# A decoder trunk with eight experts: expert stages of 2048 and 1536 features in place of 1024 and 512

## Chip, cores and metric

One core of one Trainium2 chip. The metric is the device time of one execution in microseconds; the figure for a kernel is the median of its timed runs. All arithmetic is float32.

## The reference

Two decoder layers over 256 tokens of width 1024. Each layer has a token mixer (four groups of four heads, one input and one output projection) and a channel mixer; layer 0 has a dense SwiGLU, layer 1 the expert SwiGLU that this case is about. Its part of the reference, cut to what is computed:

```python
logits = xf @ router_w + router_b                 # 256 x 8
top_logit, top_e = top_k(logits, 2); top_w = softmax(top_logit)
for each expert e, for the tokens xb that chose it:
    y = (silu(xb @ wg[e]) * (xb @ wu[e])) @ wd[e]  # wg, wu 1024 x 3584; wd 3584 x 1024
    out[token] += top_w * y
x = x + g2 * out
```

Each expert's three matrices are 14.7 MB each, so the eight experts have 352 MB of weights, and each byte is used once.

## The kernel before

**Teams.** After the router the experts are ordered by how many tokens chose them and put into eight slots of five teams (`TEAMS`, line 304): teams 0, 2 and 4 hold two experts side by side in the 128 rows of the PE array's output, teams 1 and 3 one expert. A matmul of a two-expert team is done in `lanes` of 32 or 64 rows, each lane with its own expert's weights; the lanes of one 128 x 512 product run beside each other. The rows of a team are gathered from the normalised activations by a matmul with a 0/1 matrix (`gather`) into `xT`, one of two buffers, and the results are returned to the tokens by a matmul with the transposed, weighted matrix (`moe_scatter`, line 1604), which DVE adds to the residual (`add_team`).

**Stages.** The 3584 features of a team are cut by `SPANS` into stages of 1024, 1024, 1024 and 512 features, that is 2, 2, 2 and 1 units of 512. `STAGES` is the order of the work: the stages of teams 0 and 1 alternate, then those of 2 and 3, then team 4 by itself, 20 stages. In stage j PE does: the gate sums of stage j (`moe_up(j, 0)`), with the transposes of stage j-1's products (`moe_turn`) and other small jobs (`beside`) between the pieces; the up sums (`moe_up(j, 1)`); then the down product of stage j-1 (`moe_down`), summed in banks 0 and 1 over a team's consecutive stages. Where the other team comes next, DVE takes the sums out (`run_out`) into `ysum`.

**Banks and the chain between engines.** The gate sums of a stage's two units stand in banks 4 and 2, the up sums in banks 5 and 3, transposes in 6, gathers and returns in 7. ACT takes tanh of the gate sum (`sigmoid`, line 1028), DVE multiplies it with the gate sum into `hbuf` (`gated`, 2273), and later with the up sum (`multiplied`, 2282); PE transposes `hbuf` into bank 6, ACT copies it to `hbT` (`turned_in`, 1019) for the down product. Gate and up of stage j both wait until all products of stage j-1 are made (semaphore `h`).

**Weights.** All weights come over one queue, SP's, into a ring of seven slots of 2 MB (16 KB on each of 128 partitions). `MOE_LOADS` lists the 168 expert loads in the order in which PE uses them. A gate or up load of a 2-unit stage is a piece of 512 rows by 1024 features (2 MB, runs of 4 KB); for a 1-unit stage it is all 1024 rows by 512 features (runs of 2 KB); a down load is 512 rows of 4 KB that lie together, so that each partition reads one run of 16 KB. SP waits for `ring_free` of the slot, then issues:

```python
sp.wait_ge(ring_free[slot], FREED[slot] + n // RING)
...
sp.dma_start(wide_at(slot), w[512 * piece:512 * piece + 512, st.f0:st.f0 + 1024]...)   # 2 units
sp.dma_start(view_at(slot, 512), w[:, st.f0:st.f0 + 512]...)                          # 1 unit
```

PE frees the slot of a first piece and of a down load with its last matmul on it; ACT frees gate's last piece when the gate sum is done, DVE up's. The very last down load of each of the two last experts is split into two halves, the second on semaphores of its own. The order of the experts is a result of the router, so no expert load is issued before that (`order_ready`).

**Returns.** `RETURN_IN` puts the four returns of each of teams 0 to 3 beside stages 9, 10, 17 and 18; team 4's come after the last stage, in four banks. Experts with more tokens than their slot has rows would be done in a loop at the end (`n_over`).

Of the kernel before, what the change touches and what calls it, by code (L numbers as in the profile page):

```python
# [15 lines left out]
ALU = mybir.AluOpType  # L16
# [281 lines left out]
def expert_steps(rounds):  # L298

    return [Step(w, 0, 0, [3 * u + p for p in range(3)], rounds, True, True, u == 0, u == 6)  # L300
            for u, (_, w) in enumerate(FE_UNITS)]
# [4 lines left out]
SPANS = ((0, 2), (1024, 2), (2048, 2), (3072, 1))  # L306
# [41 lines left out]
GATHER_A, GATHER_B = {2: (6, 2), 3: (8, 0), 4: (14, 2)}, {2: (7, 1), 3: (8, 2), 4: (15, 1)}  # L348
RETURN_IN = {9: 0, 10: 1, 17: 2, 18: 3}
PICKED_IN, WEIGHED_IN, TURNED_IN = {5: (2, 3), 13: (4,)}, {11: (2, 3), 13: (4,)}, {1: (0, 1), 11: (2, 3), 13: (4,)}  # L350
# [3 lines left out]
def _list_loads():  # L354
# [16 lines left out]
assert len(MOE_LOADS) == LOADS * N_EXP  # L371
# [21 lines left out]
def program(nc, t, out):  # L393
    ctx = ExitStack()
    with ctx:
# [108 lines left out]
        pickT_area = [acc[:, 1, :], bias[:, :, :].rearrange("p h n -> p (h n)")[:, 1024:1536]]  # L504
        pickT = [pickT_area[q // 2][:, 256 * (q % 2):256 * (q % 2) + 256].rearrange("p (t n) -> p t n", t=TT) for q in range(4)]
# [3 lines left out]
        ysum = [ysb, bias_flat[:, 0:1024]]  # L509
# [9 lines left out]
        def prm(l, name, p0=0, p1=128):  # L519
# [91 lines left out]
            "g", "u", "tanh", "h", "T", "T_evac", "d", "y_taken", "onehot", "turned", "turn_evac", "gathered", "in_act", "in_vec",  # L611
            "y_0", "y_1", "scattered", "added", "act_seq", "vec_seq", "act_left",
            "vec_left")} for p in ("moe", "over"))
# [26 lines left out]
        def wide_at(slot):  # L640
            return ring[:, slot, :].rearrange("p (k n) -> p k n", k=KC // 2)
# [36 lines left out]
        def _(sp):  # L678
# [82 lines left out]
            for n, (st, part, piece, m) in enumerate(MOE_LOADS):  # L761
# [4 lines left out]
                if part == 2:  # L766
                    src, c = down_rows(e, st, piece, (0,) if st is STAGES[-1] else (0, 1))
                    sp.dma_start(ring[:, slot, c], src).then_inc(ring_full[slot], 16)
                elif st.units == 2:
                    sp.dma_start(wide_at(slot), w[512 * piece:512 * piece + 512, st.f0:st.f0 + 1024].rearrange("(k p) n -> p k n", p=128)).then_inc(ring_full[slot], 16)  # L770
                else:
                    sp.dma_start(view_at(slot, 512), w[:, st.f0:st.f0 + 512].rearrange("(k p) n -> p k n", p=128)).then_inc(ring_full[slot], 16)  # L772

            for m in STAGES[-1].members:
                src, c = down_rows(expert_id(len(TEAMS) - 1, m), STAGES[-1], 0, (1,))
                sp.dma_start(ring[:, moe_slot(STAGES[-1], 2, 0, m), c], src).then_inc(ada_full[m], 16)
# [3 lines left out]
            with sp.If(n_over > 0):  # L780
                with sp.Fori(0, OVER) as i:
                    with sp.If(i < n_over):
                        e = sp.value_load(overi[0:1, bass.ds(i + (OVER + 1), 1)], min_val=0, max_val=N_EXP - 1)
                        for u in range(7):
                            for j in range(3):
                                expert_load(3 * u + j, e, u, j, i * 3 + 3 * N_EXP)
# [18 lines left out]
        def _(act):  # L805
# [213 lines left out]
            def turned_in(j, unit):  # L1019
# [6 lines left out]
                do(act.activation(hbT[:, unit, :], ps[6][:, :], ACT.Copy), moe["T_evac"])  # L1026

            def sigmoid(j, unit):
# [3 lines left out]
                if unit == st.units - 1:  # L1032
                    for m in st.members:
                        act.sem_inc(ring_free[moe_slot(st, 0, st.units - 1, m)], 1)
                if j and unit == 0:
                    act.wait_ge(moe["h"], st.at)
                do(act.activation(hsigs[unit], ps[(4, 2)[unit]][:, :], ACT.Tanh, scale=0.5), moe["tanh"])  # L1037

            for j in range(len(STAGES) + 1):
                if j:  # L1040
                    turned_in(j - 1, 0)
# [3 lines left out]
                if j and STAGES[j - 1].units == 2:  # L1045
                    turned_in(j - 1, 1)
# [18 lines left out]
        def _(pe):  # L1065
# [475 lines left out]
            def moe_up(j, part, between=None):  # L1541
# [5 lines left out]
                if j:  # L1547
                    pe.wait_ge(moe["h"], st.at)
                for piece in range(2):
                    if piece < st.units:  # L1550
                        moe_loaded(pe, st, part, piece)
                    for unit in range(st.units):
                        b = ps[((4, 2), (5, 3))[part][unit]]
                        for k in range(4 * piece, 4 * piece + 4):
                            for n, (m, c0, c1) in enumerate(st.lanes):
                                if st.units == 2:
                                    w = wide_at(moe_slot(st, part, piece, m))[:, k % 4, 512 * unit:512 * unit + 512]
                                else:
                                    w = view_at(moe_slot(st, part, 0, m), 512)[:, k, :]
                                last = mm(b[c0:c1, :], xT[st.team % 2][:, k, c0:c1], w, start=k == 0, stop=k == KC - 1)  # L1560
                                if st.units == 2 and piece == 0 and unit == 1 and k == 3 and n == st.last_lane[m]:
                                    last.then_inc(ring_free[moe_slot(st, part, 0, m)], 1)
                        if piece:
# [4 lines left out]
            def moe_turn(j, unit):  # L1568
# [5 lines left out]
                for q in range(4):  # L1574
                    c = slice(q, 512, 4)
                    last = nc.tensor.transpose(ps[6][:, 128 * q:128 * q + 128], hbuf[:, unit, c], ident)  # L1576
                last.then_inc(moe["T"], 1)

            def moe_down(j):
# [4 lines left out]
                for unit in range(st.units):  # L1584
# [3 lines left out]
                    for qs in ((0, 1), (2, 3)) if st is STAGES[-1] else ((0, 1, 2, 3),):  # L1588
# [3 lines left out]
                        for half in range(2):  # L1592
                            for q in qs:
                                for n, (m, c0, c1) in enumerate(st.lanes):
                                    slot = moe_slot(st, 2, unit, m)
                                    last = mm(ps[half][c0:c1, :], hbT[:, unit, 128 * q + c0:128 * q + c1],  # L1596
# [846 lines left out]
```

## Time and profile before

| | us |
|---|---|
| median of 3 runs | 1579.42 |
| lowest, highest | 1575.38, 1581.16 |
| the profiled execution | 1575.83 |
| its span, first to last instruction | 1574.0 |
| mean granted TensorE clock | 0.975 of full speed |
| PE busy | 1466.0 (93%) |
| DVE busy | 471.2 (30%) |
| ACT busy | 197.6 (13%) |
| HBM read | 479.41 MB, 305 GB/s over the span |

Busy shares are means over stages with different limits. The expert part runs from about 695 us, where the order of the experts is known, to about 1563 us; the rest of the time is the first layer and the second mixer, in which the change touches nothing. Times in the rows count from the first instruction.

### The profile page before, as it was taken

The numbers are of one execution on the slowest core, as the hardware profiler recorded it, in microseconds if no ns is written. First come the engines' busy times: TensorE is split into PE (matmuls) and PEld (weight loads), VectorE is DVE, ScalarE is ACT, GpSimd is POOL, SyncE is SP. The second block draws the span as 40 slices with busy tenths as digits, with TensorE's granted clock in tenths as the row PEclk, the third lists the DMA queues.
The fourth block names the chain that finished last, engine by engine and source line by source line (L and its number), as shares of the span: only waits on it lengthen the run. The fifth ranks groups of instructions, "written<-read, shape, count | busy, mean of one in ns | idle before, by whom it ended". The sixth has DMA issues, their size and how long they took to land.

```text
span 1574.0 us, 16822 instructions
## 1 busy us (share of the span) xinstructions
PE 1466.0 (93%) x6928; PEld 720.5 (46%) x6928; DVE 471.2 (30%) x937; ACT 197.6 (13%) x427; POOL 2.5 (0%) x23
## 2 busy tenths in 40 slices
PE   6899999999999999988989999999999999987886
PEld 2576755555544756662424333434343344332322
DVE  4478725344334555352100111112110110110001
ACT  1123223000003132330000000100000001000000
POOL 0000000000000000000000000000000000000000
PEclk9999989999999999989999999999999999999999
DMA  9935535887874310039999999999999999999995
GB/s 345 360 136 182 187 112 197 270 299 247 310 280 151 108 55 1 1 115 409 419 414 419 408 417 404 411 411 419 411 418 409 413 409 410 411 409 418 418 401 225
DMA packets 151647, 481.60 MB, mean 306 GB/s; under 512 B 15848, under 2 KB 33640, under 8 KB 144144
## 3 DMA queue, kind: packets, MB, share of 16 engines
q1 hardware_dynamic: 150120, 478.64, 78.4%
q10 hardware_dynamic: 1448, 1.84, 0.4%
q8 instruction: 57, 0.93, 0.2%
q14 instruction: 22, 0.18, 0.0%
HBM read 479.41 MB, written 1.06 MB: 305 GB/s over the span
## 4 chain that ended last, share of the span: by engine, by line
PE 77%; DMA 17%; DVE 2%; SPq 1%; ACT 1%; issue 1%; DVEq 0%; ACTq 0%
PE bank L1560 23%; PE bank L1596 14%; DMA ring<-in_moe_wu 13%; PE bank L1432 9%; PE bank L1190 7%; PE bank L1450 5%; PE bank L1179 4%; PE bank L1397 3%; DMA ring<-in_moe_wg 2%; DMA ring<-in_ada_w 1%; PE bank L1317 1%; PE bank L1169 1%; SPq L772 1%; PE bank L1267 1%; PE bank L1266 1%
## 5 line engine op out<-in xcount | busy, mean ns | idle before, releaser
L1560 PE MATMUL bank<-ring,h_T 128*32 128x512 f32 (+1 forms) x2240 | 310.2, 614 | 47.4 <-DMA ring<-in_moe_wu 35.3
L1596 PE MATMUL bank<-ring,m_qk_T 128*32 128x512 f32 (+2 forms) x1344 | 246.7, 596 | 12.6 <-issue 10.0
L1560 PEld LDWEIGHTS bank<-ring,h_T 128*32 128x32 f32 (+1 forms) x2240 | 99.8, 118 | 244.5 <-issue 243.4
L1560 PE MATMUL bank<-ring,cmp_region 128*128 128x512 f32 x448 | 196.3, 592 | 1.2 <-DVE m_s_region L2289 1.2
L1596 PEld LDWEIGHTS bank<-ring,m_qk_T 128*32 128x32 f32 (+2 forms) x1344 | 88.6, 128 | 166.4 <-issue 166.4
L1432 PE MATMUL bank<-ring,h_T 128*128 128x384 f32 (+1 forms) x448 | 156.8, 503 | 0.7 <-DVE m_s_region L2088 0.7
L1560 PEld LDWEIGHTS bank<-ring,cmp_region 128*128 128x128 f32 x448 | 84.0, 190 | 102.0 <-issue 102.0
L1190 PE MATMUL bank<-ring,h_T 128*128 128x512 f32 (+1 forms) x320 | 119.1, 522 | 0.8 <-ACT wide L879 0.5
L1432 PEld LDWEIGHTS bank<-ring,h_T 128*128 128x128 f32 x448 | 83.3, 190 | 61.3 <-issue 15.5
L1026 ACT ACTIVATE m_qk_T<-bank 128x512 f32<-128x512 f32 x35 | 20.9, 597 | 656.4 <-PE bank L1576 655.9
L2289 DVE SCALAR_TENSOR_TENSOR m_s_region<-m_s_region,bank 128x512 f32<-128x512 f32 x35 | 24.1, 688 | 262.1 <-PE bank L1560 262.1
L1190 PEld LDWEIGHTS bank<-ring,h_T 128*128 128x128 f32 x320 | 60.7, 196 | 43.5 <-issue 38.3
L1450 PE MATMUL bank<-ring,m_qk_T 128*128 128x512 f32 x176 | 77.9, 593 | 0.7 <-ACT m_qk_T L982 0.7
L2179 DVE SCALAR_TENSOR_TENSOR ada_acc<-ring,cond,ada_acc 128x512 f32<-128x512 f32 x98 | 73.7, 752 | 5.0
L2280 DVE SCALAR_TENSOR_TENSOR m_s_region<-s_v,bank 128x512 f32<-128x512 f32 x20 | 13.8, 688 | 155.5 <-ACT s_v L1037 155.5
L1179 PE MATMUL bank<-h_T,ring 128*128 128x256 f32 x256 | 60.3, 390 | 0.0
L1397 PE MATMUL bank<-ring,h_T 128*128 128x512 f32 x128 | 59.7, 615 | 0.0
L1179 PEld LDWEIGHTS bank<-h_T,ring 128*128 128x128 f32 x256 | 48.7, 195 | 7.7 <-ACT m_s_region L881 0.7
L1450 PEld LDWEIGHTS bank<-ring,m_qk_T 128*128 128x128 f32 x176 | 33.4, 190 | 40.2 <-issue 36.4
L2150 DVE TENSOR_TENSOR x_res<-bank,x_res 128x512 f32<-128x512 f32 x20 | 13.8, 692 | 96.0 <-PE bank L1612 95.5
L1397 PEld LDWEIGHTS bank<-ring,h_T 128*128 128x128 f32 x128 | 24.2, 197 | 25.8 <-issue 25.8
L948 ACT ACTIVATE prob<-prob,neg_max 128x128 f32<-128x128 f32 (+1 forms) x48 | 21.8, 455 | 88.5 <-DVE neg_max L1900 87.7
(355 smaller groups left out, 1041.5 us busy)
## 6 DMA issues: line engine op xcount, KB each, us to landing
ring<-in_moe_wg SPq DMA_DIRECT2D x56, 2048.0 KB, 21.2
ring<-in_moe_wu SPq DMA_DIRECT2D x56, 2048.0 KB, 21.2
ring<-in_moe_wd SPq DMA_DIRECT2D x54, 2048.0 KB, 23.1
ring<-in_ada_w SPq DMA_DIRECT2D x28, 1024.0 KB, 8.8
ring<-in_ada_w SPq DMA_DIRECT2D x10, 2048.0 KB, 14.2
ring<-in_w_in SPq DMA_DIRECT2D x10, 2048.0 KB, 10.7
ring<-in_ffn_wg SPq DMA_DIRECT2D x6, 1536.0 KB, 10.2
ring<-in_ffn_wu SPq DMA_DIRECT2D x6, 1536.0 KB, 9.0
```

The source lines that it names most:

```text
L772: sp.dma_start(view_at(slot, 512), w[:, st.f0:st.f0 + 512].rearrange("(k p) n -> p k n", p=128)).then_inc(ring_full[slot], 16)
L948: do(act.activation(e[:, a:b], e[:, a:b], ACT.Exp, bias=nmax[:, i % 4, tt:tt + 1], accum_out=lsum[:, i // H, h, tt:tt + 1]), head_exp if t ...
L1026: do(act.activation(hbT[:, unit, :], ps[6][:, :], ACT.Copy), moe["T_evac"])
L1179: last = mm(b[:, 256 * part:256 * part + 256], w[:, k, 128 * (2 * g + part):128 * (2 * g + part) + 128], hT[:, k, :], start=k == 0, stop=k ...
L1190: last = mm(b[:, 0:cols], hT[:, k, 128 * tt:128 * tt + 128], w[:, k, c0:c0 + cols], start=k == 0, stop=k == KC - 1)
L1397: last = mm(b[:, :], hT[:, k, 128 * tt:128 * tt + 128], slot_view(i, 512)[:, k, :], start=k == PAIRS_OF_K[0][0], stop=k == PAIRS_OF_K[3][1])
L1432: last = mm(ps[5 - part if f is ffn else 4 + part][:, 0:w], hT[:, k, 128 * st.tile:128 * st.tile + 128], view_at(slot, w)[:, k, :], start= ...
L1450: last = mm(ps[st.y + half][:, :], hbT[:, j % 2, 128 * q:128 * q + 128], down_at(st.slots[2], st.w)[:, q, 512 * half:512 * half + 512], st ...
L1560: last = mm(b[c0:c1, :], xT[st.team % 2][:, k, c0:c1], w, start=k == 0, stop=k == KC - 1)
L1596: last = mm(ps[half][c0:c1, :], hbT[:, unit, 128 * q + c0:128 * q + c1], down_at(slot, 512)[:, q, 512 * half:512 * half + 512], start=st.b ...
L2179: ins = STT(a, w, cond[:, 4 * i + k:4 * i + k + 1], a, ALU.mult, ALU.add)
L2289: do(STT(hbuf[:, unit, :], hbuf[:, unit, :], 0.5, ps[(5, 3)[unit]][:, :], ALU.mult, ALU.mult), moe["h"])
```

## The change

- `SPANS` has two stages for a team, of 4 and 3 units. There are 10 stages: 0 to 3 for teams 0 and 1, 4 to 7 for teams 2 and 3, 8 and 9 for team 4.
- Gate and up of every stage come in four pieces (`PIECES`) of 256 rows by all features of the stage: 2 MB in runs of 8 KB, or 1.5 MB in runs of 6 KB. Down loads are as before. There are 184 expert loads, and still seven slots.
- Gate and up sums of a unit use one bank (`GU` = 4, 2, 5, 3). PE starts a unit's up sum only after the semaphore `t`, which DVE raises when `gated` has read the gate sum. Up no longer waits for `h`.
- Four buffers each for the products and their transposes, in tiles that are idle in this part; the tanh of units 2 and 3 reuses the buffers of 0 and 1 after `t`.
- The returns of teams 0 and 1 move beside stage 8, those of teams 2 and 3 beside stage 9; each team has a `ysum` of its own until then. Gathers and the making of 0/1 matrices move with the new stage numbers.
- The loop for overfull experts starts at another ring slot (`SHIFT`).

```diff
-SPANS = ((0, 2), (1024, 2), (2048, 2), (3072, 1))
+SPANS = ((0, 4), (2048, 3))
+PIECES = 4
...
-GATHER_A, GATHER_B = {2: (6, 2), 3: (8, 0), 4: (14, 2)}, {2: (7, 1), 3: (8, 2), 4: (15, 1)}
-RETURN_IN = {9: 0, 10: 1, 17: 2, 18: 3}
+GATHER_A, GATHER_B = {2: (2, 4), 3: (4, 0), 4: (6, 4)}, {2: (3, 1), 3: (4, 4), 4: (7, 1)}
+RETURNS = {(j, hook): [(2 * (j - 8) + n // 4, n % 4) for n in pieces]
+           for j in (8, 9) for hook, pieces in enumerate(((0,), (1,), (2,), (3,), (4, 5), (6, 7)))}
+YSUM_OF = (0, 1, 2, 3, 0)
...
-                for piece in range(STAGES[j].units):
+                for piece in range(PIECES):
                     add(STAGES[j], part, piece)
...
+        hbufs = [hbuf[:, 0, :], hbuf[:, 1, :], gate[:, 0, 0:512], gate[:, 0, 512:1024]]
+        hbTs = [hbT[:, 0, :], hbT[:, 1, :], cmp_region[:, 1024:1536], cmp_region[:, 1536:2048]]
+        GU = (4, 2, 5, 3)
...
+                    sp.dma_start(wide_at(slot, st.units), w[256 * piece:256 * piece + 256, st.f0:st.f0 + 512 * st.units].rearrange("(k p) n -> p k n", p=128)).then_inc(ring_full[slot], 16)
...
-                if j and unit == 0:
+                if unit >= 2:
+                    act.wait_ge(moe["t"], st.at + unit - 1)
+                elif j:
                     act.wait_ge(moe["h"], st.at)
-                do(act.activation(hsigs[unit], ps[(4, 2)[unit]][:, :], ACT.Tanh, scale=0.5), moe["tanh"])
+                do(act.activation(hsigs[unit % 2], ps[GU[unit]][:, :], ACT.Tanh, scale=0.5), moe["tanh"])
...
-                if j:
+                if j and part == 0:
                     pe.wait_ge(moe["h"], st.at)
...
+                for piece in range(PIECES):
+                    moe_loaded(pe, st, part, piece)
                     for unit in range(st.units):
-                        b = ps[((4, 2), (5, 3))[part][unit]]
-                        for k in range(4 * piece, 4 * piece + 4):
+                        if part and piece == 0:
+                            pe.wait_ge(moe["t"], st.at + unit + 1)
+                        b = ps[GU[unit]]
+                        for k in range(2 * piece, 2 * piece + 2):
...
-                do(STT(hbuf[:, unit, :], hsigs[unit], 1.0, ps[(4, 2)[unit]][:, :], ALU.add, ALU.mult))
+                do(STT(hbufs[unit], hsigs[unit % 2], 1.0, ps[GU[unit]][:, :], ALU.add, ALU.mult), moe["t"])
```

## Rows read from the trace of the kernel before

**Rows 1.** The page's slices of 39.4 us (PE's busy tenths, granted clock, DMA, GB/s):

```profile
PE   6899999999999999988989999999999999987886
...
PEclk9999989999999999989999999999999999999999
DMA  9935535887874310039999999999999999999995
GB/s 345 360 136 182 187 112 197 270 299 247 310 280 151 108 55 1 1 115 409 419 414 419 408 417 404 411 411 419 411 418 409 413 409 410 411 409 418 418 401 225
```

**Rows 2.** Who waits for whom (us in total, times, longest), PE's and SP's rows:

```profile
PE bank L1560 <- DMA ring<-in_moe_wu: 35.3, 15, 4.6
...
PE bank L1560 <- DMA ring<-in_moe_wg: 12.1, 8, 2.6
...
PE bank L1596 <- DMA ring<-in_moe_wd: 1.8, 1, 1.8
...
PE bank L1560 <- DVE m_s_region L2289: 1.2, 1, 1.2
...
SPq L770 <- PE bank L1560: 106.1, 19, 10.1
SPq L770 <- PE bank L1596: 88.5, 16, 7.0
SPq L770 <- DVEq L2288: 64.2, 12, 9.3
...
SPq L770 <- ACTq L1034: 47.0, 9, 7.7
```

**Rows 3.** Windows: stretch, length, busy us and counts of each engine, clock, DMA share, GB/s:

```profile
core 0: us, PE busy (x) PEld busy (x) DVE busy (x) ACT busy (x) POOL busy (x), PEclk, DMA share, GB/s
697.00:1556.00 859.00, 796.89 (x4344) 315.46 (x4344) 113.69 (x225) 50.94 (x90) 0.00 (x0) 0.98 1.02 411
705.00:745.00 40.00, 31.79 (x261) 12.37 (x264) 9.64 (x30) 3.02 (x6) 0.00 (x0) 0.91 1.02 409
755.00:775.00 20.00, 20.00 (x57) 9.71 (x56) 2.44 (x4) 2.39 (x4) 0.00 (x0) 1.00 1.02 428
970.00:980.00 10.00, 10.00 (x100) 2.99 (x92) 1.38 (x2) 0.00 (x0) 0.00 (x0) 1.00 1.05 387
1546.00:1549.00 3.00, 1.61 (x8) 0.74 (x10) 0.00 (x0) 0.00 (x0) 0.00 (x0) 1.00 1.02 423
5.00:6.00 1.00, 0.00 (x0) 0.00 (x0) 0.00 (x0) 0.00 (x0) 0.00 (x0) 1.00 0.99 401
```

**Rows 4.** Times from issue to landing, line 770: the first load, then 710 to 1500 us:

```profile
L770 SPq DMA_DIRECT2D ring<-in_moe_wg x1: 397/397/397, 695.6 to 695.6; - x1
...
DMA to landing us min/median/max: 7.6/7.6/7.6
...
L770 SPq DMA_DIRECT2D ring<-in_moe_wu x47: 372/2699/6452, 705.1 to 1461.7; - x47
...
L770 SPq DMA_DIRECT2D ring<-in_moe_wg x44: 372/384/6004, 722.7 to 1441.8; - x44
...
DMA to landing us min/median/max: 11.4/21.8/29.0
```

**Rows 5.** Chain of waits in order: start, us, what (counts include weight loads):

```profile
696.76 13.01 DMA ring<-in_moe_wg
...
764.22 13.74 PE bank L1560 x32
777.96 13.87 PE bank L1596 x128
...
849.40 0.47 PE bank L1576 x4
849.87 6.87 PE bank L1560 x16
...
992.43 1.98 PE bank L1497 x16
...
1015.48 1.78 PE bank L1497 x16
...
1087.95 0.86 PE bank L1612 x2
...
1234.54 8.77 PE bank L1560 x64
...
1424.68 7.10 PE bank L1560 x32
```

**Rows 6.** Groups by line, 697 to 1556 us: names, count, busy us, mean ns, idle:

```profile
L1026 ACT ACTIVATE m_qk_T<-bank 128x512 f32<-128x512 f32 x35 | 20.9, 597 | 656.4 <-PE bank L1576 655.9
...
L2280 DVE SCALAR_TENSOR_TENSOR m_s_region<-s_v,bank 128x512 f32<-128x512 f32 x20 | 13.8, 688 | 155.5 <-ACT s_v L1037 155.5
L1037 ACT ACTIVATE s_v<-bank 128x512 f32<-128x512 f32 x20 | 11.9, 597 | 83.7 <-PE bank L1560 83.7
L2150 DVE TENSOR_TENSOR x_res<-bank,x_res 128x512 f32<-128x512 f32 x16 | 11.1, 692 | 95.1 <-PE bank L1612 94.7
```

**Rows 7.** The same chain at its end:

```profile
1547.39 7.09 PE bank L1596 x32
1554.47 0.69 PE bank L1576 x4
...
1555.25 0.60 ACT m_qk_T L1026
...
1555.99 7.09 PE bank L1596 x32
1563.08 3.65 PE bank L1612 x8
```

More of the change, by code:

```diff
@@ L1044, in _ @@
                         sigmoid(j, unit)
-                if j and STAGES[j - 1].units == 2:
-                    turned_in(j - 1, 1)
+                for unit in units[PIECES - 1:]:
+                    turned_in(j - 1, unit)
                 for team, (at, _) in GATHER_A.items():
@@ L1546, in moe_up @@
                     pe.wait_ge(moe["in_vec"], st.team + 1)
-                if j:
+                if j and part == 0:
                     pe.wait_ge(moe["h"], st.at)
-                for piece in range(2):
-                    if piece < st.units:
-                        moe_loaded(pe, st, part, piece)
+                for piece in range(PIECES):
+                    moe_loaded(pe, st, part, piece)
                     for unit in range(st.units):
-                        b = ps[((4, 2), (5, 3))[part][unit]]
-                        for k in range(4 * piece, 4 * piece + 4):
+                        if part and piece == 0:
+                            pe.wait_ge(moe["t"], st.at + unit + 1)
+                        b = ps[GU[unit]]
+                        for k in range(2 * piece, 2 * piece + 2):
                             for n, (m, c0, c1) in enumerate(st.lanes):
[L1556 to L1563, printed above, removed]
+                                slot = moe_slot(st, part, piece, m)
+                                last = mm(b[c0:c1, :], xT[st.team % 2][:, k, c0:c1], wide_at(slot, st.units)[:, k % 2, 512 * unit:512 * unit + 512],
+                                          start=k == 0, stop=k == KC - 1)
+                                if piece < PIECES - 1 and unit == st.units - 1 and k % 2 and n == st.last_lane[m]:
+                                    last.then_inc(ring_free[slot], 1)
+                        if piece == PIECES - 1:
                             last.then_inc(moe["gu"[part]], 1)
@@ L1574, in moe_turn @@
                 for q in range(4):
-                    c = slice(q, 512, 4)
-                    last = nc.tensor.transpose(ps[6][:, 128 * q:128 * q + 128], hbuf[:, unit, c], ident)
+                    last = nc.tensor.transpose(ps[6][:, 128 * q:128 * q + 128], hbufs[unit][:, q:512:4], ident)
                 last.then_inc(moe["T"], 1)
@@ L1587, in moe_down @@
                     end = st.end and unit == st.units - 1
-                    for qs in ((0, 1), (2, 3)) if st is STAGES[-1] else ((0, 1, 2, 3),):
+                    for qs in ((0, 1), (2, 3)) if st is STAGES[-1] and end else ((0, 1, 2, 3),):
                         if qs[0]:
@@ L1644, in _ @@
                     moe_up(j, 1)
-                    beside(j, 2)
+                    beside(j, 4)
                 else:
-                    moe_turn(j - 1, 0)
+                    for unit in range(STAGES[-1].units):
+                        moe_turn(j - 1, unit)
                 if j:
@@ L1650, in _ @@
                 if j < len(STAGES):
-                    beside(j, 3)
+                    beside(j, 5)
             for n in range(4):
@@ L2130, in run_out @@
                     c = slice(512 * half, 512 * half + 512)
-                    y = ysum[st.team % 2][:, c]
+                    y = ysum[YSUM_OF[st.team]][half]
                     if half:
```

87 lines of the change are left out of this document (44 added, 43 removed).

## The prediction

> **What bounds the kernel now.** I read the page's 40 slices first [rows 1]: from slice 18 on, which is the expert part, the DMA row stands at 9 with some 410 GB/s in every slice but the last, while PE is at 8 or 9 too. Two candidates, so the next view is who waits for whom in this stretch [rows 2]: PE waits for weight loads 35.3 + 12.1 + 1.8 us and for almost nothing else, and SP, which issues the loads, waits far longer for PE, ACT and DVE to free a ring slot. So the loads run ahead until the seven slots are full, and the question is whether the queue ever runs dry. It doesn't: from 697 to 1556 us the rate is 411 GB/s with a DMA share of 1.02 [rows 3], and between 710 and 1500 us a gate or up load takes 11.4 to 29.0 us from issue to landing, where the first one, with nothing ahead of it, took 7.6 [rows 4]; there is always more than one load in the queue. 352.3 MB of expert weights at 411 GB/s are 857 us. PE needs less: one unit of 512 features costs 24 matmuls of 0.86 us and a transpose, 6.87 + 6.87 + 6.93 + 0.47 = 21.1 us [rows 5], whether the team has one expert or two, since the strips of two experts run side by side; 35 units are 739 us. The expert part is bound by its loads, from first to last, and PE has 100 us to spare in the sum. But not everywhere: a unit of a one-expert team is loaded in 3 x 4.9 to 5.1, 15 us, and computed in 21.1; a unit of a two-expert team is loaded in 30 and computed in 21.1. The one-expert stages are PE's, the others are the queue's, and the ring has to bridge them. That is where I look at this change.
>
> **Part 1: longer rows of gate and up weights (a gain).** Of gate and up, 96 loads came as 4 KB rows (201.3 MB) and 16 as 2 KB rows (33.6 MB); down weights come as 16 KB. Stretches that hold one kind only, by the order and times of SP's issues [rows 3]: 4 KB rows 409 GB/s, 2 KB rows 387, 16 KB rows 428. Per packet on one of 16 engines that is 2048 x 16/387 = 84.7 ns, 4096 x 16/409 = 160.2, 16384 x 16/428 = 612.5. Twice the first less the second leaves 9.2 ns that don't depend on size; (4 x 160.2 - 612.5)/3 leaves 9.4. So 9.3 ns for each packet. Before, 49,152 + 16,384 packets; after, the 4-unit stages have 64 loads of 256 rows x 8 KB (16,384 packets) and the 3-unit stages 64 of 256 rows x 6 KB (16,384). 32,768 fewer, 2048 an engine, x 9.3 ns = **19.0 us less**. The bounds: if rows over 4 KB ran at 409, only the 2 KB loads gain, 33.6 MB x (1/387 - 1/409) = 4.7 us; if at 428, the 201.3/409 + 33.6/387 = 579.0 us of before become 234.9/428 = 548.8, 30 less. The constants at the start are rows of 6272 B and ran at 401 GB/s in a ramping microsecond, the two half loads of 8 KB rows at the end at 423 [rows 3]; both are nearer to my value than to either end.
>
> The same fixed part has a page. The Trainium skill (DMA: Bandwidth & Descriptors, "Why small descriptors are slow") puts it at about 3 cycles a packet, and its section on the 436 GB/s has 850 MHz: an estimate of 3.5 ns, by which this part would give 7.2 us and not 19.0. The trace does not agree: 9.2 and 9.4 ns from two pairs of rows. A small fixed part stays in as a rival.
>
> **Part 2: stages of 4 and 3 units (a loss).** The longer a one-expert stage, the further PE falls behind the queue, and the ring holds seven slots as before. If it fills, the queue stands idle from the freeing of a slot to the next load's first byte. I keep a ledger. A load can start when the one before it has ended and the seventh before it has been freed r us ago; r lies between 0 and 7.6 - 5.1 = 2.5 us, all that an unqueued load takes beside its transfer [rows 4]; part of that is after the last byte, so I take 1.5. Loads: 4.9 us for 2 MB in 16 KB rows, 5.0 in 8 KB rows, 3.8 for 1.5 MB in 6 KB rows. PE: 6.87 us for a piece of 4 units or for a unit of down, 5.15 for a piece of 3 units, 0.47 for a transpose after a piece, 1.8 to 2.0 for half a gather [rows 5].
>
> Stage 5 (one expert, 4 units), from T, where team 2's last up piece has landed: PE frees the slots in order at T+15.7, 22.6, 29.4 (down of stage 3, behind 6.9 of up and 2 of gather), 36.3, 43.6, 51.0, 58.3 (gate), 65.1, 72.0, 78.9, 85.7 (up), then 92.6, two at a time. The queue has ended all 11 of these loads by T+53.7, and now brings down weights of stage 4: those that end at 58.6, 63.5, 68.4, 73.3 go through, the fifth waits for 72.0 + 1.5 (0.2 us lost), the next for 78.9 + 1.5 (2.0), 85.7 + 1.5 (1.9), and the first of stage 6 for 92.6 + 1.5 (2.0): **6.1 us of idle queue**. Stages 3 and 7 (one expert, 3 units, behind 27.5 us of down for the 4 units of stages 1 and 5): gate frees at T+39.7, 45.3, 52.6, 58.2, up at 63.4, 68.5, 73.7, 78.8, down at 85.7; the queue is at 48.9 when the pair's down loads begin, and loses 0.3 + 0.7 + 0.3 + 0.2 + 0.3 + 0.2 + 1.9 = **3.9 us each**. Stage 1 has no down of a one-expert team ahead of it: 0. Sum 6.1 + 2 x 3.9 = **13.9 us lost**; with r = 0 it is 9.4, with r = 2.5 16.9. The same ledger for the kernel before never fills: two units put PE 12 us behind, two and a half of the slots.
>
> **Part 3: gate and up share a bank.** PE may start the up sum of a unit when its gated sum is written, which is tanh 0.60 us, multiply 0.69 [rows 6] and some 0.2 us of semaphores after the gate sum: 1.5 us. Gate sums of a last piece end 1.72 us apart, and up starts with unit 0, whose gate sum is then 5.2 us old (3.4 with 3 units); unit 3 is needed 5.2 us after its own end. Cost 0, covered by the other units' matmuls. If DVE came late by more than 3.7 us, PE would pay in full (the rival below). DVE is busy 114 of 859 us here [rows 3].
>
> **Part 4: what is moved.** The 16 returns of teams 0 to 3 (0.86 us on PE [rows 5], 0.69 on DVE [rows 6]) go to stages 8 and 9, of a two-expert team, where a piece has 10.0 us of loads to 6.9 of PE: 0. The pairs at hooks 4 and 5 share bank 7, so the second waits 0.8 us for DVE's add; behind it stand down's matmuls, which have slack in these stages. They leave stage 9 of before, a one-expert stage: nothing, since its ring didn't fill. Fewer sums are run out through DVE (off the path). SP issues 186 loads and not 170, at 0.4 us each [rows 4], against 3.8 us or more of transfer for each: 0. Loads start at the same moment (the expert order), and PE's first piece still needs 4 MB: 0. At the end, both kernels are held by PE: before, from the landing of stage 18's last down load, 6.9 + 1.6 (transpose, eviction) + 6.9 = 15.4 us against 9.8 of loads, so 5.6 behind the last landing [rows 7]; after, 6.9 + 2.5 (two returns) + 4.6 (three transposes with evictions) + 20.6 = 34.6 against 29.4: 5.2. Within the error, 0.
>
> **The sum.** -19.0 + 13.9 = -5.1 us. The profiled execution took 1575.83 (span 1574.0), so 1570.7; it was near the lowest of the three timed runs (1575.38 to 1581.16). Against their median 1579.42 the forecast is **1574.3 us**, 0.3% less, and a run set of this kernel can't tell less than 0.5% (7.9 us) from no change.
>
> **Rivals.**
> (a) The queue doesn't starve. If the freeing of slots ran some 10 us ahead of my ledger, all of the 19 us shows: 1560.4. For it: no load of the expert part but the first found an empty queue in this trace, so nothing there shows what a refill costs. Against: PE's rates in the ledger are the chain's own. 0.20.
> (b) Slower: the shared bank holds PE up in one-expert stages. Place: the start of up in stages 3, 5 and 7, whose ring is full; price: if DVE or ACT is caught behind a turned pick, a gather's eviction or a run-out, up to 1.5 us a unit, 10 units, 15 us, and each microsecond there goes straight out of the queue: -19.0 + 13.9 + 15 = +10, 1589.3. It decides once the chain is 3.7 us late. Against: DVE's list there is short. 0.12.
> (c) Long rows give half: either the fixed part doesn't shrink with the count of packets above 4 KB as it does below, or the 6 KB rows are cut into 4 + 2 KB packets, 16,384 more, which takes 9.5 us back. -9.5 + 13.9 = +4.4: 1583.8. Against: both ways of taking 9.3 ns agree up to 16 KB, and 6272 B rows ran at 401. 0.12. By the 3 cycles of the Trainium skill (DMA: Bandwidth & Descriptors, "Why small descriptors are slow") it would be an estimated 1586.1.
> (d) My forecast, 0.56, with its own range: r from 0 to 2.5, and 17 to 20 of gain: -10.6 to -0.1, and 2 to 3 us more for pieces that PE runs slower after an idle (8.77 where others take 7.07 [rows 5]): 1568.8 to 1582.3.
>
> Faster by over 0.5% (under 1571.5): (a) and a fifth of (d), 0.31. Slower (over 1587.3): (b) and little of (c), 0.13. Same 0.56. For 8 in 10 the range must reach half into (a) and (c): 1562 to 1587.
>
> **What would show it.** Right: packets of 8 and 6 KB at 417 to 421 GB/s; slices of the DMA row at 10 to 15% less near the ends of stages 3, 5 and 7 (about 980 to 1010, 1160 to 1190, 1300 to 1340 us), with landing times there near 7.6 us; PE without idle in them; no wait of PE on DVE at up. Wrong: a flat rate to the end (a); PE waits on DVE at the up line (b); 409 GB/s in the gate and up stretches (c).

## The result, and the profile after

The changed kernel is slower: 1585.5 us (1583.23 to 1589.16 in 8 runs) against 1576.6 for the kernel before on the same chip (1574.79 to 1581.16 in 8). The ratio is 1.0054 with an interval of 1.0041 to 1.0067, that is 8.5 us. The forecast was 0.3% faster. The time lies in the range, the sign is wrong.

The profiled execution took 1589.16 us, span 1587.3, mean granted clock 0.974. It is 13.3 us over that of before, and 3.1 of these lie ahead of the expert part: its first load was issued at 698.7 us here and at 695.6 before. From there to the start of the last four returns it is 877.5 us here and 867.5 before.

The slices of the page, 39.7 us each (compare [rows 1]):

```profile
span 1587.3 us, 16812 instructions
...
PE   5999999999999999986799899988999899979987
...
PEclk9999989999999999989999999999999999999999
DMA  9935526877873400039999999999989999999996
GB/s 346 354 134 194 190 94 211 279 270 278 310 280 112 145 16 1 1 147 421 420 425 380 417 422 392 387 421 424 424 316 416 422 412 356 422 424 378 413 428 255
DMA packets 119135, 481.60 MB, mean 303 GB/s; under 512 B 16104, under 2 KB 33896, under 8 KB 95248
```

The page of before had 151,647 packets for the same bytes, 32,512 more. Where the queue runs it now brings 412 to 428 GB/s, in ten of the slices 420 to 425, where before it brought 401 to 419; but in five places slices are far below that, and no full slice of before's expert part was under 401. The reader should see both: a level that rose by 2 to 3%, and holes. The same in windows of one kind of load (length, busy us and counts of each engine, clock, DMA share, GB/s), first 8 KB rows, then 6 KB rows, then stretches of 40 us:

```profile
core 0: us, PE busy (x) PEld busy (x) DVE busy (x) ACT busy (x) POOL busy (x), PEclk, DMA share, GB/s
750.00:780.00 30.00, 21.22 (x192) 7.16 (x192) 0.69 (x1) 0.48 (x1) 0.00 (x0) 1.00 1.01 422
890.00:925.00 35.00, 28.84 (x244) 9.65 (x235) 2.07 (x3) 2.98 (x5) 0.00 (x0) 0.95 1.02 419
820.00:860.00 40.00, 40.00 (x173) 16.28 (x175) 4.13 (x6) 1.79 (x3) 0.00 (x0) 1.00 0.95 386
980.00:1020.00 40.00, 40.00 (x199) 15.41 (x201) 5.76 (x10) 1.90 (x4) 0.00 (x0) 1.00 0.97 372
1140.00:1180.00 40.00, 40.00 (x103) 18.03 (x105) 4.80 (x7) 3.58 (x6) 0.00 (x0) 1.00 0.89 357
1180.00:1220.00 40.00, 40.00 (x368) 12.48 (x364) 4.35 (x11) 1.19 (x2) 0.00 (x0) 1.00 0.95 380
1300.00:1340.00 40.00, 40.00 (x142) 18.51 (x144) 5.75 (x10) 2.98 (x5) 0.00 (x0) 1.00 0.95 369
1460.00:1500.00 40.00, 40.00 (x182) 13.86 (x180) 6.64 (x10) 4.18 (x7) 0.00 (x0) 1.00 0.93 373
```

In each of the low ones PE is busy for all 40.00 us: it is the bound there, and the queue waits for it. (Some matmul records of 1140 to 1180 us are missing, so its count is low.) Taken against 421 GB/s, a 40-us window at rate R has lost 40 x (1 - R/421) us. With the neighbouring windows that are low (a row of them for all kernels stands below), stage 1 lost 3.3, stage 3 6.2, stage 5 10.0, stage 7 6.6 and stage 9 4.6: 30.7 us.

The waits of the expert part (compare [rows 2]) say where the bound isn't. PE's columns are the total, the times, the longest:

```profile
PE bank L1567 <- DMA ring<-in_moe_wu: 34.0, 15, 2.9
...
PE bank L1567 <- DMA ring<-in_moe_wg: 15.7, 9, 3.3
...
PE bank L1619 <- DVE x_res L2158: 3.8, 4, 1.0
...
PEld bank L1567 <- DVE gate_rows L2288: 0.5, 2, 0.2
...
SPq L778 <- PE bank L1567: 226.8, 32, 11.1
```

PE waits for loads as before (49.7 us against 47.4), 0.5 us in two waits for `gated` (L2288) at the start of an up sum, and 3.8 us for DVE between returns. SP's longest waits are for PE's gate and up matmuls (226.8 us; before, 106.1 on L770 and 13.5 more on L772, the line of the 1-unit loads). Such a wait says only that the ring is full, which it was before too [rows 2]; that the queue ran dry is seen in the rates.

### The profile page after: what moved, and what is told of

It reads as the page before. It is cut to its first block, busy times and chain, and to the rows that moved or that the text cites. A ratio compares the mean times of both kernels' runs of the same rounds, so it can differ in the third digit from the quotient of the medians.

```text
span 1587.3 us, 16812 instructions
## 1 busy us (share of the span) xinstructions
PE 1467.5 (92%) x6928; PEld 722.1 (45%) x6928; DVE 460.1 (29%) x921; ACT 197.6 (12%) x427; POOL 2.5 (0%) x23
## 4 chain that ended last, share of the span: by engine, by line
PE 79%; DMA 15%; DVE 2%; issue 1%; ACT 1%; SPq 1%; DVEq 0%; ACTq 0%
PE bank L1567 22%; PE bank L1603 15%; PE bank L1441 9%; PE bank L1199 7%; DMA ring<-in_moe_wu 7%; DMA ring<-in_moe_wg 6%; PE bank L1459 5%; PE bank L1188 4%; PE bank L1406 3%; DMA ring<-in_ada_w 1%; DMA ring<-in_moe_wd 1%; PE bank L1619 1%; PE bank L1326 1%; PE bank L1583 1%; PE bank L1178 1%
## 5 line engine op out<-in xcount | busy, mean ns | idle before, releaser
L1603 PE MATMUL bank<-ring,m_qk_T 128*32 128x512 f32 (+2 forms) x768 | 141.1, 598 | 2.3 <-DMA ring<-in_moe_wd 1.4
L1441 PEld LDWEIGHTS bank<-ring,h_T 128*128 128x128 f32 x448 | 83.3, 190 | 61.3 <-issue 15.5
L1603 PE MATMUL bank<-ring,cmp_region 128*32 128x512 f32 (+2 forms) x576 | 106.7, 599 | 3.7 <-issue 3.7
L1603 PEld LDWEIGHTS bank<-ring,m_qk_T 128*32 128x32 f32 (+2 forms) x768 | 50.3, 129 | 89.4 <-issue 89.3
L2297 DVE SCALAR_TENSOR_TENSOR m_s_region<-m_s_region,bank 128x512 f32<-128x512 f32 x20 | 13.8, 688 | 251.6 <-PE bank L1567 251.6
L1032 ACT ACTIVATE m_qk_T<-bank 128x512 f32<-128x512 f32 x20 | 11.9, 597 | 595.0 <-PE bank L1583 595.0
L1199 PEld LDWEIGHTS bank<-ring,h_T 128*128 128x128 f32 x320 | 60.7, 196 | 43.5 <-issue 38.3
L1603 PEld LDWEIGHTS bank<-ring,cmp_region 128*32 128x32 f32 (+2 forms) x576 | 38.8, 129 | 70.0 <-issue 70.0
L2288 DVE SCALAR_TENSOR_TENSOR m_s_region<-s_v,bank 128x512 f32<-128x512 f32 x10 | 6.9, 688 | 163.6 <-ACT s_v L1045 163.6
## 6 DMA issues: line engine op xcount, KB each, us to landing
ring<-in_moe_wg SPq DMA_DIRECT2D x32, 1536.0 KB, 13.5
```

The lines of the kernel that those rows point to most:

```text
L1199: last = mm(b[:, 0:cols], hT[:, k, 128 * tt:128 * tt + 128], w[:, k, c0:c0 + cols], start=k == 0, stop=k == KC - 1)
L1441: last = mm(ps[5 - part if f is ffn else 4 + part][:, 0:w], hT[:, k, 128 * st.tile:128 * st.tile + 128], view_at(slot, w)[:, k, :], start= ...
L1603: last = mm(ps[half][c0:c1, :], hbTs[unit][:, 128 * q + c0:128 * q + c1], down_at(slot, 512)[:, q, 512 * half:512 * half + 512], start=st. ...
```

## The experiments

Two theories went in. **A**: the ring fills in the one-expert stages and the queue runs dry, for more than the ledger's 13.9 us. **B**: long rows are worth less than 19 us, or the loss is in the returns, the clock or the long stage as such. Every figure below is a median beside its ratio to the kernel before; a ratio's hundredth of a per cent is 0.16 us. A difference between two kernels of this list is uncertain by 2 to 3 us. The part ahead of the experts has a share in that: the first expert load is issued between 692.3 and 699.7 us in the kept traces, though nothing is changed ahead of it. So here is also the expert part of each trace alone, from that issue to the start of the last four returns; it is one execution of each, against a median in the text below:

| | expert part, us | less than before | less than the changed kernel |
|---|---|---|---|
| before | 867.5 | | |
| changed | 877.5 | -10.0 | |
| half of one-expert work, changed kernel | 849.1 | 18.4 | 28.4 |
| half of one-expert work, kernel before | 867.7 | -0.2 | |
| no returns | 878.1 | | -0.7 |
| long stages, 4 and 2 KB rows | 894.7 | -27.2 | |
| only team 4 long | 861.9 | 5.6 | |
| 3, 2, 2 | 860.5 | 7.0 | 17.0 |
| two-expert teams long | 863.0 | 4.5 | |
| PE kept busy | 875.6 | | 1.9 |
| stage 1 halved | 872.7 | | 4.7 |
| 3 and 7 halved | 866.8 | | 10.7 |
| 5 halved | 869.3 | | 8.2 |
| 3, 2, 2, returns spread | 859.7 | 7.8 | |

**Half of PE's work in the one-expert stages, in the changed kernel and in the one before.** All loads stay.

```diff
-                        for k in range(2 * piece, 2 * piece + 2):
+                        for k in range(2 * piece, 2 * piece + len(st.members)):
...
-                    for qs in (... else ((0, 1, 2, 3),)):
+                    for qs in (... else ((0, 1, 2, 3)[0:2 * len(st.members)],)):
```

> The changed kernel, with half of PE's work in one-expert stages left out (every second k of gate and up, two of four q of down), all loads as they are. Theory A (the queue runs dry because PE falls behind in one-expert stages): PE can't fall behind any more, the queue idles nowhere, and the 19 us of the longer rows show: about 1557 to 1560 us, 25 us under the changed kernel. Rival B (the shared bank stalls PE, or the moved work does): the time stays above 1575, since the stalls at the banks and the moved returns stay. Rival C (long rows give little): half_after equals half_before within 5 us.

> The kernel before with the same half of PE's work left out in one-expert stages. All theories: the queue was never dry, so nothing changes but at most 1 us (1575 to 1577). The difference to half_after is the worth of the longer rows alone: 19 us by A, under 8 by C.

Measured: 1558.52, 0.9875 [0.9859, 0.9892] for the changed kernel with half the work, and 1576.49, 0.9995 [0.9985, 1.0005] for the kernel before with half the work. The pair settles the account. With PE out of the way the two kernels differ by 0.0120, **18.9 us** (18.6 by the two expert parts): that is what the longer rows are worth, together with whatever the moved returns, the shared bank and the new end cost in this state; the forecast had 19.0. PE's work in one-expert stages cost the kernel before 0.8 us, which can't be told from nothing, and costs the changed one 28.2, so the change made **27.4 us** of new dependence on PE. 27.4 - 18.9 = 8.5, the result. The flat rate is to be seen in one window of each, first the changed kernel's. Its loads end earlier, and the window has some of their end in it; from 700 to 1500 us the rates are 422 and 413 GB/s, 9 apart, and 352.3 MB take 18.2 us less at the first:

```profile
700.00:1540.00 840.00, 678.62 (x4004) 262.00 (x4006) 102.53 (x208) 50.94 (x90) 0.00 (x0) 0.95 1.01 420
```

```profile
700.00:1540.00 840.00, 675.19 (x3948) 258.67 (x3949) 110.43 (x208) 50.34 (x89) 0.00 (x0) 0.94 1.02 413
```

**No returns of teams 0 to 3.** Left out in stages 8 and 9.

```diff
-           for j in (8, 9) for hook, pieces in enumerate(((0,), (1,), (2,), (3,), (4, 5), (6, 7)))}
+           for j in () for hook, pieces in enumerate(((0,), (1,), (2,), (3,), (4, 5), (6, 7)))}
```

> The changed kernel with the returns of teams 0 to 3 left out (16 matmuls on PE and 16 adds on DVE in stages 8 and 9). In the trace of the changed kernel the queue idles some 4 us in stage 9 behind them. Theory A: 4 us under the changed kernel (1581), since the idle of stages 1, 3, 5 and 7 stays. Rival B in the form that the moved returns are the loss: 10 us or more less (1575 or under).

Measured: 1581.15, 1.0029 [1.0015, 1.0043], 3.9 us less than the changed kernel, with some 3 us of uncertainty. The returns were costed at nothing. Stage 9's hole goes with them; the profiled execution was the slowest of its ten (1586.29 us), though, its holes in stages 3, 5 and 7 are deeper, and its expert part is no shorter, so that the trace shows the place and the median the size; from 1457 to 1483 us, the changed kernel and then the one without returns:

```profile
1457.00:1483.00 26.00, 25.92 (x114) 9.07 (x116) 6.22 (x9) 2.98 (x5) 0.00 (x0) 1.00 0.88 344
```

```profile
1457.00:1483.00 26.00, 25.47 (x121) 9.46 (x118) 2.07 (x3) 4.18 (x7) 0.00 (x0) 1.00 1.02 417
```

**Long stages with rows of 4 and 2 KB.** The 4-unit stages load two units at a time, the 3-unit stages two units and then one.

```diff
-PIECES = 4
+PLANS = {4: (((0, 1), 0, 4), ((0, 1), 4, 8), ((2, 3), 0, 4), ((2, 3), 4, 8)), 3: (((0, 1), 0, 4), ((0, 1), 4, 8), ((2,), 0, 8))}
```

> The changed kernel with its stages of 4 and 3 units, shared banks and returns, but with the rows of before: a load is 512 rows of 1024 features (4 KB rows), for the third unit of a 3-unit stage 1024 rows of 512 features (2 KB rows), 168 loads. Theory A (long stages cost 27 us by a dry queue, long rows gain 18): no gain and the whole loss, 25 to 29 us over the kernel before, 1602 to 1606, and the same number over half_before. Rival B' (the loss comes with the 6 KB loads that fill only 1.5 of a slot's 2 MB): the slots are full here, so half of the loss is gone, 1588 to 1594.

Measured: 1600.62, 1.0153 [1.0135, 1.0170], 24.1 us slower than before and 15.6 slower than the changed kernel. Of the two expectations it is 1.4 us under A's and 6.6 over the rival's. The two parts of the change come apart: the stages cost, the rows give back. The other idea on record, that the 6 KB loads lose because they fill only three quarters of a slot, falls with it.

**Only team 4 in long stages.** Teams 0 to 3 stay at 2, 2, 2, 1 units.

```diff
+ORDER_OF_STAGES = ((0, 2), (1, 2), (0, 2), (1, 2), (0, 2), (1, 2), (0, 1), (1, 1), (2, 2), (3, 2), (2, 2), (3, 2), (2, 2), (3, 2), (2, 1), (3, 1), (4, 4), (4, 3))
```

> Teams 0 to 3 in stages of 2, 2, 2 and 1 units with the rows of before, team 4 (two experts) in stages of 4 and 3 with 8 and 6 KB rows; banks shared and returns in team 4's stages as in the changed kernel. Theory A: no one-expert stage is long, so nothing is lost but up to 4 us behind the returns, and two of eight experts gain: 18/4 = 4.5 us, so 0 to 5 us under the kernel before, 1572 to 1577. If sharing the banks cost something by itself, it would be over 1580.

Measured: 1570.03, 0.9963 [0.9948, 0.9978], 5.8 us less than before, 2 us under the expected band. Team 4 has a quarter of the packets that the change saves, 8192 of 32,768, 512 an engine x 9.3 ns = 4.8 us. Where no one-expert stage is long, the rows' gain shows whole.

**Stages of 3, 2 and 2 units for teams 0 to 3, team 4 as changed.**

```diff
+ORDER_OF_STAGES = ((0, 3), (1, 3), (0, 2), (1, 2), (0, 2), (1, 2), (2, 3), (3, 3), (2, 2), (3, 2), (2, 2), (3, 2), (4, 4), (4, 3))
+PIECES_OF = {4: 4, 3: 4, 2: 2, 1: 1}
```

> The changed kernel with stages of 3, 2 and 2 units for teams 0 to 3 (6 KB rows in four pieces, 4 KB rows in two) and 4 and 3 for team 4; shared banks, t waits and all else kept. Theory A: PE falls at most 18 us behind in a one-expert stage, the ring doesn't empty, and what is left of the longer rows shows: 11 to 14 us under the kernel before, 1563 to 1566. Rival B (shared banks cost): at or above the kernel before, 1577 or more.

Measured: 1566.55, 0.9926 [0.9909, 0.9943], 11.7 us less than before and 20 less than the changed kernel: **the version that beats both**. It saves 12 x 1024 packets in teams 0 to 3 and 8192 in team 4, 20,480, 1280 an engine x 9.3 ns = 11.9 us. By the medians next to nothing of its gain is lost again. The expert part says 7.0 us and not 11.7, which would leave 4.9 lost, and the windows have room for that: a hole at 980 us, in a one-expert stage of 2 units (3.4 us against 421 GB/s), and a shallow one at 1420 us:

```profile
980.00:1020.00 40.00, 40.00 (x193) 17.53 (x195) 5.08 (x9) 2.39 (x4) 0.00 (x0) 1.00 0.95 385
1140.00:1180.00 40.00, 36.39 (x332) 11.61 (x324) 2.75 (x4) 2.39 (x4) 0.00 (x0) 1.00 1.03 408
1420.00:1460.00 40.00, 39.05 (x146) 14.36 (x144) 7.60 (x11) 2.98 (x5) 0.00 (x0) 1.00 1.00 405
```

**Long stages for the two-expert teams, shorter ones for the others.** The one-expert team of a pair has 3, 2, 2 units, the last two one behind the other.

```diff
+ORDER_OF_STAGES = ((0, 4), (1, 3), (0, 3), (1, 2), (1, 2), (2, 4), (3, 3), (2, 3), (3, 2), (3, 2), (4, 4), (4, 3))
```

> Two-expert teams in stages of 4 and 3 units (8 and 6 KB rows), one-expert teams in 3, 2 and 2 (6 and 4 KB rows), in the order pair 4, single 3, pair 3, single 2, single 2. Theory A: most of the longer rows' gain (15 us) and 2 to 4 us of dry queue: 1562 to 1566, under spans322 (1566.6) or level with it. If long stages cost by their length in any team, it would be well above spans322.

Measured: 1572.04, 0.9980 [0.9966, 0.9993]: a miss, 6 us above the band. Its packets (28,672 fewer) are worth 16.7 us by the same count and 3.2 showed. I had looked at the size of a stage and not at the number of one-expert units in a row. By the windows (all against 421 GB/s) some 13 us are lost: 3.4 at team 1's two stages of 2 units (385 GB/s from 1020 to 1060 us), 5.9 at team 3's (1260 to 1380 us), and 3.8 at team 3's stage of 3 units (1100 to 1180 us). So stages in a row do add up, but a 3-unit stage loses as well, behind a two-expert stage of 4. These are that stage, and team 3's last two:

```profile
1140.00:1180.00 40.00, 40.00 (x247) 14.45 (x249) 2.07 (x3) 0.00 (x0) 0.00 (x0) 1.00 0.98 389
1300.00:1380.00 80.00, 80.00 (x362) 31.23 (x352) 6.90 (x10) 3.58 (x6) 0.00 (x0) 1.00 0.97 394
```

How much of this belongs to the row of stages and how much to the longer two-expert stages was not taken apart; the rival on record, that a long stage costs in any team, is not excluded here.

**PE kept busy in the waits of two-expert stages**, stage 4 being the one looked at. After an idle the clock of the changed kernel was at 0.66 of full speed from 1083 to 1092 us (a mix of the 1.2 and the 2.4 GHz level), in the matmuls that end stage 4. If that lateness made the hole behind it, extra matmuls in the waits would close it.

```profile
1083.00:1092.00 9.00, 8.90 (x56) 2.55 (x60) 0.00 (x0) 0.00 (x0) 0.00 (x0) 0.66 1.03 428
```

```diff
+                    if part and len(st.members) > 1 and piece < PIECES - 1:
...
+                        for _ in range(2):
+                            mm(ps[6][:, :], ident, const[:, 0:512], start=True, stop=True)
```

> The changed kernel with two 128x512 matmuls more (1.7 us, into the transposes' bank) after each of the first three up pieces of two-expert stages, where PE waits 2.6 to 3 us for loads. In the trace of the changed kernel the clock fell to 0.66 in 1083 to 1092 us and two pieces took 17.0 us instead of 14.1, just before a one-expert stage. If that late start is part of the loss, 3 to 5 us less than the changed kernel (1581 to 1582). If the idle queue needs no late start, no change (1585).

Measured: 1586.47, 1.0069 [1.0051, 1.0086], no gain. The clock from 1060 to 1100 us was 0.87 in the changed kernel and is 1.00 here; PE enters stage 5 some 1.6 us earlier, counted from the first expert load. The hole stayed, 9.3 us in two windows where it was 10.0. The expert part is 1.9 us shorter in the one execution that was traced, which is less than the 3 to 5 us that would have been a part of the loss, and can't be told from nothing:

```profile
1060.00:1100.00 40.00, 37.13 (x280) 14.14 (x272) 4.39 (x8) 0.00 (x0) 0.00 (x0) 1.00 1.01 425
1140.00:1180.00 40.00, 40.00 (x136) 17.30 (x139) 5.50 (x8) 3.58 (x6) 0.00 (x0) 1.00 0.88 348
```

**Half of PE's gate and up work in single stages**: stage 1, stages 3 and 7, stage 5 of the changed kernel. The down products keep all their work here; in the pair above they were halved too.

```diff
-                        for k in range(2 * piece, 2 * piece + 2):
+                        per = 1 if j in (3, 7) else 2
+                        for k in range(2 * piece, 2 * piece + per):
```

> The changed kernel, with every second k of gate and up left out in stage 1 alone (one expert, 4 units; 27 us of PE), all loads as they are. My ledger lost nothing there: by it no change (1585.5). By the ledger with the lag of landings behind the queue that the traces show (2.4 us or more, where I had 1): 3 to 4 us less, 1581.5 to 1582.5.

> The same in stages 3 and 7 (one expert, 3 units). By my ledger 7.8 us less (1577.7); by the corrected one 11 to 13 us less (1572.5 to 1574.5).

> The same in stage 5 (one expert, 4 units, behind down weights of a 3-unit stage). By my ledger 6.1 us less (1579.4); by the corrected one 8 to 10.5 us less (1575 to 1577.5). If the three halved kernels together save 27 less 4 us, the dry queue of the one-expert stages is the whole of the loss but for the returns.

| | median | ratio | less than the changed kernel | the prediction's ledger | by the windows |
|---|---|---|---|---|---|
| stage 1 halved | 1583.71 | 1.0049 [1.0033, 1.0064] | 0.8 | 0 | 3.3 |
| 3 and 7 halved | 1573.58 | 0.9984 [0.9974, 0.9993] | 11.0 | 7.8 | 12.8 |
| 5 halved | 1578.99 | 1.0014 [1.0000, 1.0029] | 6.3 | 6.1 | 10.0 |
| no returns | 1581.15 | 1.0029 [1.0015, 1.0043] | 3.9 | 0 | 4.6 |

The last column is what each place lost in the changed kernel's trace. The timed effects sum to 22.0, 18.1 of it for the stages, and all one-expert work together gave 28.2. The expert parts of the traces give the three stage edits 4.7, 10.7 and 8.2, 23.6 together. Rates of 40-us windows from 780 us on (each edit closes its own hole; the others stay, earlier by what was saved):

```
stage            1         3           5              7                9
         780 820 | 940 980 | 1140 1180 | 1260 1300 1340 | 1420 1460 1500
changed  422 386 | 405 372 |  357  380 |  419  369  403 |  418  373  429
1        424 423 | 393 382 |  342  405 |  416  360  422 |  391  415  429
3 and 7  421 387 | 419 423 |  325  396 |  418  426  421 |  373  415  428
5        424 393 | 391 386 |  425  417 |  380  374  423 |  373  425  427
returns  424 395 | 379 376 |  331  377 |  419  353  406 |  421  419  428
```

With stages 3 and 7 halved, stage 5 lost 11.5 us in place of 10.0; with 5 halved, stage 7 lost 8.4 in place of 6.6. That would be some 3 of the missing 6 us, given back because the queue arrives further ahead. But it is a hint and no more: stage 3's hole, which the edit of the returns doesn't touch, was 8.3 in that trace and 6.2 in the changed kernel's, and the four differences together are uncertain by some 5 us. The halved down products of the pair are another candidate, and by the expert parts little is missing (23.6 and the returns' 3.9 against 28.4). What the sum lacks stays open.

**3, 2, 2 with the returns spread out.** Team 0 is returned beside the two-expert stage 8 already, team 1 beside stages 10 and 12, one return per hook.

```diff
+RETURNS = {(8, 0): [(0, 0)], (8, 1): [(0, 1)], (8, 4): [(0, 2)], (8, 5): [(0, 3)], (10, 0): [(1, 0)], (10, 1): [(1, 1)], (12, 0): [(1, 2)], (12, 1): [(1, 3)], ...}
```

> spans322 with the 16 returns one to a hook, beside stages 8, 10, 12 and 13 (all of two-expert teams), where spans322 has two thirds of them beside stage 12 and 13 with pairs that wait for DVE. no_returns saved 4.4 us against the changed kernel, and spans322 shows the same dip of the queue (405 GB/s in 1420 to 1460 us). If that dip is the returns' bunching, 2 to 4 us under spans322: 1562.5 to 1564.5. If it is the number of returns, no change (1566.5).

Measured: 1568.98, 0.9954 [0.9939, 0.9968]: a miss, 4 us above the band, and 4.4 above the version with the returns in stages 12 and 13 (uncertain by some 3.5 us). The late hole closed and there is one in front, at 1140 us:

```profile
1140.00:1180.00 40.00, 40.00 (x356) 12.41 (x352) 4.14 (x6) 2.39 (x4) 0.00 (x0) 1.00 1.00 389
1420.00:1460.00 40.00, 40.00 (x148) 14.97 (x146) 7.51 (x11) 2.99 (x5) 0.00 (x0) 1.00 1.01 417
...
1144.00:1148.00 4.00, 4.00 (x44) 1.20 (x40) 0.00 (x0) 0.00 (x0) 0.00 (x0) 1.00 0.78 262
...
L1623 PE MATMUL bank<-f_qk_T,ada_acc x8: 592/593/697, 1165.4 to 1216.1; 128*128 128x512 f32 x8
```

It is tempting to say that the returns moved it there. They didn't: the first return of this kernel (L1623, the last line shown) starts at 1165.4 us, the lowest rate is at 1144 to 1148, and up to that return the two kernels do the same. One execution gave 408 GB/s from 1140 to 1180 us and the other 389, with the same work behind them (the second began its expert part 2.1 us later), and each single window in this document is to be read with that in mind. The expert parts are 859.7 and 860.5 us, so the traces don't show the 4.4 us either. Spreading the returns brought none of the 2 to 4 us hoped for; that it costs anything is not shown.

## Why the prediction was wrong

**What bounds the kernel**: right. Halving PE's one-expert work moved the kernel before by 0.8 us, which can't be told from nothing: its expert part was the queue's alone.

**Part 1, longer rows, 19.0 us**: right, 18.9 by the pair with half the work, with 2 to 3 us of uncertainty. 8 KB rows ran at 422 GB/s and 6 KB rows at 419, forecast 417 to 421. Rival (c), with 9.5 us, fell. By the small fixed part of the Trainium skill (DMA: Bandwidth & Descriptors, "Why small descriptors are slow") it would have been an estimated 7.2; the runs don't agree.

**Part 2, the dry queue, 13.9 us**: this is the step that failed, by its size; the mechanism and its places were right. Rival (a), no starving, fell with the five holes. With the returns' 3.9 taken from the 27.4, the stages cost some 23.5; the stages halved one at a time gave 18.1 by the medians and 23.6 by the expert parts, all above 13.9. Stage 5 shows the ledger at work. These are SP's issues of stage 4's down loads (minimum, median, maximum ns, first and last start) and their time to landing:

```profile
L776 SPq DMA_DIRECT2D ring<-in_moe_wd x6: 332/333/333, 1152.2 to 1187.1; - x6
...
DMA to landing us min/median/max: 8.5/8.7/9.9
```

Six issues are 34.9 us from first to last, five periods of 7.0, which is PE's 6.87 for a slot; the transfers are 4.9 each. That leaves 34.9 - 24.5 = 10.4 us, less some 1.2 for the first load, which still had a transfer ahead of it (9.9 us to landing where the other five took 8.5 to 8.8): about 9 us lost where the ledger had 6.1, and 10.0 by the windows. The timed effect of halving this stage, 6.3, is as the ledger had it; its trace says 8.2. So of the single stages it is not this one that shows the miss clearly, but 3 and 7 (11.0 and 10.7 against 7.8) and the total.

What was too small in it, worked out afterwards:

- The queue's lead. The ledger set the last landing T of a two-expert stage 1 us behind the start of the next stage's first load. In the trace it is more. Below, the windows up to stage 0's and stage 2's last load, and the chain of waits at the two landings (start, us, what):

```profile
698.00:780.00 82.00, 59.80 (x513) 26.73 (x513) 18.65 (x75) 6.04 (x12) 0.00 (x0) 0.95 0.99 409
698.00:924.00 226.00, 194.88 (x1333) 78.09 (x1333) 32.64 (x99) 15.00 (x27) 0.00 (x0) 0.97 0.99 409
```

```profile
759.80 22.63 DMA ring<-in_moe_wu
...
782.57 8.45 PE bank L1567 x64
...
791.23 0.70 DVE gate_rows L2297
...
792.18 7.11 PE bank L1567 x16
...
908.62 17.21 DMA ring<-in_moe_wu
```

Stage 0's 16 loads are 33.55 MB, at 409 GB/s done at 780.0, and the last landed at 782.4; the 92.3 MB up to the end of stage 2 were done at 923.7, and landed at 925.8. So a landing is 2.1 to 2.4 us behind the bytes, and in this time the queue runs on. The ledger redone with 2.4 in place of 1 gives 5.3 for each of stages 3 and 7, 7.5 for stage 5 and still 0 for stage 1: 18.1 in all. That landing trails the bytes agrees with the Trainium skill (DMA: Bandwidth & Descriptors, "Anatomy of one DMA", written for another issuing path), by which each DMA has some 2 us of fixed cost, most of it the receipt behind the last byte.

- PE's own times. Behind stage 0's last landing PE took 8.45 us for a piece that the ledger has at 6.87, and then stood 1.2 us, 0.70 of it for DVE's last product, before stage 1 began. With PE's times as the trace has them and the lead of 2.4, the ledger gives 3.7 for stage 1, 5.8 and 6.0 for stages 3 and 7 and 8.8 for stage 5: 24.3, where the pair and the returns leave 23.5. The 24.3 is an estimate from the trace, and no run changes the lead or these delays alone.
- The refill. The 1.5 us that the ledger used for r hold: down loads that find the queue all but empty take 3.6 to 3.9 us beside their transfer, and with 2.1 to 2.4 of these behind the last byte some 1.5 are left ahead of the first. But 2.5 was no bound for what an unqueued load takes, and so 16.9 none for the loss.

Stage 1 was put at 0. Its trace has a hole of 3.3 us; halving it closed the hole and gave 4.7 us by the expert part, but 0.8 us by the medians, which can't be told from nothing.

**Part 3, the shared bank, 0**: right. PE waited 0.5 us in all for DVE at up, where rival (b) needed 15. It fell, though its time, 1589.3, is near what was measured. A forecast of the sign by (b) would have been right for a wrong reason.

**Part 4, the moved returns, 0**: wrong by 3.9 us, as far as the medians tell. "Slack in these stages" held for stages 8 and 9 as a whole, but not for their start. PE comes out of the down product of one-expert stage 7 late, and the returns keep it late, with the ring full: eight of 0.86 us or more from the last four of stage 8 on, and two of the four waits for DVE's adds, 0.9 us each. The chain has the place:

```profile
1478.70 5.30 PE bank L1567 x24
...
1484.68 0.86 PE bank L1619 x2
1485.54 10.46 PE bank L1567 x47
```

That the end and the 186 issues of SP cost nothing was not tried by itself; what they cost stands inside the 18.9, which is uncertain by 2 to 3 us.

**The sum.** -19.0 + 13.9 + 0 was forecast; -18.9 + 23.5 + 3.9 was measured. Against the medians of these runs that is 8.5 us slower. The uncertainty that decided was that of Part 2. Its range varied r alone, 9.4 at none and 16.9 at what one unqueued load at the start of the part took, of another row length; the queue's lead and PE's delays behind a late landing had no range at all. The 23.5 is what the other terms leave, so that this sum closes by its making; that the term is over 13.9 is what the runs show.

## What to carry to other kernels

When one queue feeds an engine that is by turns the faster and the slower, count the slower engine's work in a row (21.1 us for each 15 us of loads here) against what the ring holds, and look at it before a larger tile is chosen: one-expert stages of 3, 2 and 2 units with seven slots lost nothing by the medians and some 5 us by the trace, those of four and three lost 23. A longer row is worth 9.3 ns for each packet that it saves on an engine, and can be had alone, by lengthening only where the ring doesn't fill. An idle engine's time isn't free at the edge of its own bound stage: the returns put beside stages 8 and 9 met a PE that was still late from stage 7.

## What the runs showed of the hardware

- The fixed part of a packet, 9.3 ns, held from 2 KB to 16 KB rows: 387, 409, 419, 422 and 428 GB/s at 2, 4, 6, 8 and 16 KB, and 18.9 us for 2048 packets an engine.
- A 2 MB load of 16 KB rows on a queue that is all but empty took 8.5 to 8.8 us to land, 3.6 to 3.9 of them beside its transfer; the first load of the expert part took 7.6 before and 7.9 in the changed kernel. On a full queue two landings were 2.1 and 2.4 us behind the bytes.
- Extra matmuls in PE's waits lifted the granted clock of 1060 to 1100 us to 1.00 from 0.87 and changed the time by nothing that can be measured.
